# Norms whose epsilon comes from one more column: GpSimd keeps only the power

## The chip, the cores and the metric

The kernel runs on one core of one Trainium2 chip. The time is the device time of one launch in microseconds (us). The core has five engines that run their own streams of instructions and wait for each other by semaphores: TensorE (PE; its weight loads are PEld), VectorE (DVE), ScalarE (ACT), GpSimd (POOL) and SyncE (SP, which here only issues DMAs).

## The reference

256 tokens of 1,024 float32 channels go through a two-layer block (attention mixers and convolution-gated FFNs) and through a second block (gated delta rule, long convolution, FFN, a per-layer gate). What matters here are the RMS norms between them:

```python
def rms_norm(x, g):
    xf = x.astype(jnp.float32)
    y = xf * lax.rsqrt(jnp.mean(xf * xf, axis=-1, keepdims=True) + EPS)     # EPS = 1e-6
    return (y * g.astype(jnp.float32)).astype(x.dtype)

h = x
for layer in range(DEPTH):                                # 2 layers
    h = h + mixer(rms_norm(h, norm_mix_g[layer]))         # norms 0 and 2
    h = h + conv_gated_ffn(rms_norm(h, norm_ffn_g[layer])) # norms 1 and 3
h = rms_norm(h, norm_out_g)                               # norm 4
x = h + second_mixer(rms_norm_2(h, g_mix))                # norm 5
x = x + ffn(rms_norm_2(x, g_ffn))                         # norm 6
x = x + sigmoid(rms_norm_2(x, g_pl) @ w_pl_gate) * pl     # norm 7
return rms_norm_2(x, g_final)                             # norm 8
```

## The kernel before, in words

The tokens are two tiles of 128 (`t` = 0 and 1, `TT` = 2), with the tokens in the partitions of `x` and of `xn`, both `[128, 2, 1024]`. Every product is made from three matmuls (lines 1019 to 1021): each operand is kept as a rounded part (`whi`, `xhi`, `hhi`) and the rest (`wlo`, `xlo`, `hlo`). The weights come as a stream of slots from SyncE's queue into a ring `raw`; ScalarE rounds a slot into `whi` (line 1661), VectorE subtracts into `wlo` (line 2150). Each engine's program is written out in order by hand, and each instruction waits for events (semaphores of the dictionary `S`).

A norm `k` of tile `t` runs over four engines, in this order:

1. ScalarE: `square(k, t)` (line 1687) squares `x[:, t, :]` and sums into `sumsq[:, t]`. The squares themselves land in `xn`, which is free at that time, or for norm 4 in `junk_4`, a view of the convolution's tile `cv`.
2. GpSimd: `deviation(k, t)` waits for that, calls `rstd_of`, which makes `sumsq / 1024 + EPS` with a `tensor_scalar` (line 897), waits for its own semaphore (`link`), and raises it to the power -0.5 with a `tensor_tensor` (line 898) into `rstd[:, t]`.
3. VectorE: `normalize` (line 2176) writes `xn = x * rstd * gain` in two halves of 512 columns.
4. TensorE: `turn_norm` transposes `xn` in eight blocks of 128 (line 1035) into PSUM. ScalarE rounds them into `xhi` (line 1741), VectorE subtracts into `xlo` (line 2236), and the next product can begin. Around it TensorE runs filler matmuls of `ident` (`spin`, line 1026), a fixed number for each place.

Norm 0 stands behind the load of `x` at the start. Norms 1 and 3 (`norm_behind_out`) stand behind the output products of the mixers: both tiles become ready at the same time, tile 0 is normalized first. Norms 2, 4, 6 and 7 (`norm_behind_down`) stand behind down products that finish tile 0 first: its norm runs while TensorE is still at tile 1, and tile 1's norm runs while TensorE is at the next product of tile 0. Norm 5 is normed from norm 4's result with a second chain on GpSimd (`deviation_5`, lines 910 to 917), and for it `scale_x` (line 2253) rewrites `x`. Norm 8 is the last work; after it `xn` is stored tile by tile (line 874).

`rstd_of` has three other callers: `deviation_5`, the keys' layer norm and the norm of `pl`.

Of the kernel before, what the change touches and what calls it, by code (L numbers as in the profile page):

```python
# [274 lines left out]
class Event:  # L275
# [13 lines left out]


EVENTS = {

    "weights_high": "slot n's rounded weights are written",
    "weights_low": "slot n's remainders are written, its raw weights no longer needed",
# [298 lines left out]
def build(nc, dram, counted, stop=None):  # L593
# [7 lines left out]
    with ctx:  # L601
# [16 lines left out]
        raw = sb("raw", [P, RAW, SLOT])  # L618
        whi = sb("whi", [P, RING, SLOT], F32R)
        wlo = sb("wlo", [P, RING, SLOT], F32R)  # L620
        x = sb("x", [P, TT, D])
        xn = sb("xn", [P, TT, D])
        xhi = sb("xhi", [P, KT, TOK], F32R)
        xlo = sb("xlo", [P, KT, TOK], F32R)
        gain = sb("gain", [P, D])
# [13 lines left out]
        with ExitStack() as area:  # L639
            hhi = sb("hhi", [P, FT, TOK], F32R, area)  # L640
            hlo = sb("hlo", [P, FT, TOK], F32R, area)
            cv = sb("cv", [P, 2, 2, TOK], F32, area)
            sg = sb("sg", [P, 2, TOK], F32, area)
            hf = sb("hf", [P, 2, TOK], F32, area)
        with ExitStack() as area:
            temp = sb("temp", [P, 2, TT, 512], F32, area)
            rope_a = sb("rope_a", [P, 512], F32, area)
            rope_b = sb("rope_b", [P, 512], F32, area)
            v0 = sb("v0", [P, TT, 512], F32, area)
            v1 = sb("v1", [P, TT, 512], F32, area)  # L650
            fm = sb("fm", [P, 4, 4, TOK], F32, area)
            fmi = sb("fmi", [P, 3, TOK], F32, area)
            bias = sb("bias", [P, 8, 384], F32, area)
            picked = sb("picked", [P, TT, TOK], F32, area)
            score = sb("score", [P, TT, TOK], F32, area)
            rel = sb("rel", [P, 2, TOK], F32, area)
            prob = sb("prob", [P, 3, 3 * P], F32, area)
            probT = sb("probT", [P, 2, 3 * P], F32, area)
            mixed = sb("mixed", [P, 2, TT, 4 * HD], F32, area)
            mhi = sb("mhi", [P, KT, TOK], F32R, area)  # L660
            mlo = sb("mlo", [P, KT, TOK], F32R, area)
            ks = sb("ks", [P, 3, TT, 64], F32, area)
            key_mean = sb("key_mean", [P, TT], F32, area)
            key_var = sb("key_var", [P, TT], F32, area)
            key_rstd = sb("key_rstd", [P, TT], F32, area)
            index_w = sb("index_w", [P, TT, 4], F32, area)
            top8 = sb("top8", [P, 8], F32, area)
            gate = sb("gate", [P, 4, TT * 8], F32, area)
            lowest = sb("lowest", [P, 2, 4, TT], F32, area)
            total = sb("total", [P, 2, 4, TT], F32, area)  # L670
            sunk = sb("sunk", [P, 2, 4, TT], F32, area)
            inverse = sb("inverse", [P, 2, 4, TT], F32, area)
            nsink = sb("nsink", [P, 8], F32, area)
# [152 lines left out]

            return (i % 2, i // 2) if (layer, b) == ("odd", 0) else (i // 2, i % 2)

        junk_4 = cv[:, :, :, :].rearrange("p a m c -> p (a m c)")

        def summed(n, t):

            return S["weights_used"].at(n) if t else S["first_summed"].at(n)
# [26 lines left out]
        @block.sync  # L860
        def _(sp):
            sp.dma_start(ident, dram["ident"]).then_inc(ident_loaded, 16)
            for t in range(TT):
                sp.dma_start(x[:, t, :], dram["x"][t * P:(t + 1) * P, :]).then_inc(x_loaded[t], 16)
                if t == 0:
                    sp.dma_start(gain[:, :], dram["gains"][0:1, :].broadcast_to([P, D])).then_inc(gain_0_loaded, 16)
            for n in range(len(plan)):
                if n >= RAW:

                    sp.wait_ge(*weights_low(n - RAW))  # L870
                sp.dma_start(used(raw, n), weights_of(n, dram["stream"][n])).then_inc(weights_loaded[n % RAW], 16)
            for t in range(TT):
                sp.wait_ge(*S["normed"].at((NORMS - 1, t)))
                sp.dma_start(dram["out"][t * P:(t + 1) * P, :], xn[:, t, :]).then_inc(stored, 16)
            sp.wait_ge(stored, 16 * TT)


# [1 line left out]
        def _(pool):  # L879
# [20 lines left out]
            def deviation(k, t):  # L900

                pool.wait_ge(*S["squared"].at((k, t)))
                if k:
                    pool.wait_ge(*S["normed"].at((k - 1, t)))
                ins = rstd_of(rstd[:, t:t + 1], sumsq[:, t:t + 1], 1.0 / D, EPS)
                ins.then_inc(*S["rstd_ready"].one((k, t)))
                if k == 4:
                    pool.wait_ge(*S["rstd_ready"].at((k, t)))

# [8 lines left out]
            def norm(k):  # L918

                for t in range(TT):  # L920
                    deviation(k, t)

            link(pool.memset(half_power[:, :], -0.5))
            norm(0)
            pool.dma_start(cst1[:, :], dram["consts1"]).then_inc(consts_loaded, 16)
# [725 lines left out]
        def _(act):  # L1651
# [21 lines left out]
            def square(k, t):  # L1673

                if k == 0:
                    act.wait_ge(x_loaded[t], 16)
                elif k == 5:
                    act.wait_ge(*S["gained"].at((t, 1)))
                    act.activation(junk_4, xn[:, t, :], ACT.Square, accum_out=sumsq_5[:, t:t + 1])\
                        .then_inc(*S["squared"].one((5, t)))  # L1680
                    return
                else:
# [1 line left out]
                    act.wait_ge(*S["rstd_ready"].at((k - 1, t)))  # L1684

                    act.wait_ge(*S["norm_turned"].at(("o" if k == 6 else k - 1, t, 1)))
                act.activation(junk_4 if k == 4 else xn[:, t, :], x[:, t, :], ACT.Square, accum_out=sumsq[:, t:t + 1])\  # L1687
                    .then_inc(*S["squared"].one((k, t)))
                if k == 4:
                    act.wait_ge(*S["squared"].at((k, t)))  # L1690
# [1170 lines left out]
```

## Time and profile before

| | |
|---|---|
| median of three runs | 1335.07 us (1334.74 to 1338.38) |
| the profiled execution | 1332.6 us, span of its instructions 1330.8 us |
| busy in it | TensorE 97%, its weight loads 89%, VectorE 63%, ScalarE 53%, GpSimd 18% |
| chain that ended last, by engine | TensorE 89%, VectorE 5%, ScalarE 3%, GpSimd 0% (rounded) |
| line 1687, square of one tile, 1,024 columns | 1.06 us, its sum's read 0.19 us |
| line 897, scaled sum on GpSimd | 20 times, 18 of them on `sumsq` or `sumsq_5` |
| line 898, power on GpSimd | 20 times |
| line 2176, half of a tile of `xn` | 0.75 us |

The busy share of an engine alone does not say what a saved instruction is worth; for that the waits of the engine behind it are read, place by place. In the rows below a time is in microseconds from the span's start, and what stands in brackets behind an instruction is how long its engine sat idle before it and what ended that.

### The profile page before, as it was taken

The page shows a single profiled execution, that of the slowest core. Times are in us where ns is not written, and L with a number is a line of the kernel's source. Part 1 is how long each engine was busy: PE and PEld are TensorE (multiplying, and loading weights), DVE is VectorE, ACT ScalarE, POOL GpSimd, SP SyncE. Part 2 cuts the span into 40 slices and gives each one's busy share as a digit, 9 for nine tenths or more (in the row PEclk, how much of TensorE's full clock was granted, in tenths as well). Part 3 has the DMA queues.
Part 4 walks back from the last instruction along what each step waited for, and adds up shares of the span by engine and source line. Part 5 has one row for each costly group of instructions (what it writes and reads, how often), then busy time and mean ns, then how long its engine had stood idle before and what let it go on. Part 6 is the DMA issues. An engine that isn't in the chain of part 4 may idle for free.

```text
span 1330.8 us, 21614 instructions
## 1 busy us (share of the span) xinstructions
PE 1289.0 (97%) x8824; PEld 1179.5 (89%) x8824; DVE 840.3 (63%) x1454; ACT 703.6 (53%) x1161; POOL 241.9 (18%) x196
## 2 busy tenths in 40 slices
PE   8999999999999999999999999999899999999996
PEld 7777899998877789998889999999889989999875
DVE  6774487774664458776467787778843456555445
ACT  5555466553445546654355666666646335444344
POOL 2000000000000010000046665565435201000001
PEclk9999999999999999999989999999999999999999
DMA  8523355445442245545433322332202536455432
GB/s 317 215 100 122 112 190 177 178 179 182 164 152 102 89 176 219 185 175 198 143 127 127 128 96 98 125 126 97 96 33 98 182 139 216 182 190 189 175 143 79
DMA packets 31442, 200.29 MB, mean 151 GB/s; under 512 B 4272, under 2 KB 6464, under 8 KB 8560
## 3 DMA queue, kind: packets, MB, share of 16 engines
q1 hardware_dynamic: 29360, 189.79, 39.5%
q0 software_dynamic: 1840, 8.60, 1.6%
q8 instruction: 70, 1.15, 0.3%
q10 hardware_dynamic: 144, 0.52, 0.1%
q14 instruction: 28, 0.23, 0.1%
HBM read 197.85 MB, written 1.05 MB: 149 GB/s over the span
## 4 chain that ended last, share of the span: by engine, by line
PE 89%; DVE 5%; ACT 3%; issue 1%; DMA 0%; POOL 0%; SPq 0%; POOLq 0%; DVEq 0%; ACTq 0%
PE ps L1019 25%; PE ps L1021 24%; PE ps L1020 24%; PE ps L1174 2%; PE ps L1377 2%; PE ps L1142 1%; PE ps L1393 1%; DVE conv L2526 1%; PE ps L1035 1%; PE ps L1155 1%; PE ps L1333 1%; PE ps L1100 1%; DVE wlo L2150 1%; PE ps L1338 1%; PE ps L1399 1%
## 5 line engine op out<-in xcount | busy, mean ns | idle before, releaser
L1019 PE MATMUL ps<-xhi,whi 128*128 128x256 f32 x1536 | 441.3, 287 | 2.6 <-DVE xlo L2233 2.6
L1020 PE MATMUL ps<-xlo,whi 128*128 128x256 f32 x1536 | 436.3, 284 | 0.0
L1021 PE MATMUL ps<-xhi,wlo 128*128 128x256 f32 x1536 | 436.2, 284 | 0.0
L2150 DVE TENSOR_TENSOR wlo<-raw,whi 128x2048 fp32r<-128x2048 f32 (+2 forms) x144 | 324.7, 2257 | 124.5 <-ACT whi L1661 121.2
L1661 ACT ACTIVATE whi<-raw 128x2048 fp32r<-128x2048 f32 (+2 forms) x144 | 270.7, 1882 | 117.0 <-PE ps L1021 112.7
L1019 PEld LDWEIGHTS ps<-xhi,whi 128*128 128x128 f32 x1536 | 296.1, 193 | 2.9 <-DVE xlo L2233 2.8
L1020 PEld LDWEIGHTS ps<-xlo,whi 128*128 128x128 f32 x1536 | 296.1, 193 | 0.1
L1021 PEld LDWEIGHTS ps<-xhi,wlo 128*128 128x128 f32 x1536 | 295.8, 193 | 0.0
L977 POOL TENSOR_TENSOR wlo<-raw,whi 128x1024 fp32r<-128x1024 f32 x72 | 173.8, 2422 | 60.8 <-ACT whi L1670 60.5
L897 POOL TENSOR_SCALAR sumsq<-sumsq 128x1 f32<-128x1 f32 x18 | 5.8, 322 | 890.5 <-ACT xn L1687 700.9
L1019 PE MATMUL ps<-whi,xhi 128*128 128x512 f32 (+4 forms) x432 | 152.2, 352 | 4.0 <-DVE xlo L2236 3.4
L1021 PE MATMUL ps<-whi,xlo 128*128 128x512 f32 (+4 forms) x432 | 147.1, 341 | 0.0
L1020 PE MATMUL ps<-wlo,xhi 128*128 128x512 f32 (+4 forms) x432 | 146.9, 340 | 0.0
L1019 PE MATMUL ps<-whi,hhi 128*128 128x512 f32 x264 | 104.5, 396 | 0.9 <-DVE hf L2469 0.9
L1020 PE MATMUL ps<-wlo,hhi 128*128 128x512 f32 x264 | 104.4, 395 | 0.0
L1021 PE MATMUL ps<-whi,hlo 128*128 128x512 f32 x264 | 104.4, 395 | 0.0
L1019 PEld LDWEIGHTS ps<-whi,xhi 128*128 128x128 f32 x432 | 82.2, 190 | 19.9 <-issue 10.0
L2589 DVE SCALAR_TENSOR_TENSOR ps<-glu_in,par,ps 128x256 f32<-128x256 f32 x224 | 94.6, 482 | 0.0
L1833 ACT ACTIVATE cv<-ps,par 128x256 f32<-128x256 f32 x88 | 44.9, 561 | 89.6 <-PE ps L1021 83.2
L1021 PEld LDWEIGHTS ps<-whi,xlo 128*128 128x128 f32 x432 | 82.3, 191 | 9.3
L1020 PEld LDWEIGHTS ps<-wlo,xhi 128*128 128x128 f32 x432 | 82.5, 191 | 7.7
L1670 ACT ACTIVATE whi<-raw 128x1024 fp32r<-128x1024 f32 x72 | 76.1, 1060 | 11.8 <-PE ps L1021 11.8
(296 smaller groups left out, 1757.4 us busy)
## 6 DMA issues: line engine op xcount, KB each, us to landing
raw<-in_stream SPq DMA_DIRECT2D x176, 1024.0 KB, 4.8
gain<-in_gains POOLq DMA_DIRECT2D x7, 512.0 KB, 5.4
bias<-in_rel POOLq DMA_DIRECT2D x1, 1536.0 KB, 8.9
raw<-in_stream SPq DMA_DIRECT2D x2, 648.0 KB, 7.9
cst<-in_consts POOLq DMA_DIRECT2D x1, 1280.5 KB, 6.2
raw<-in_stream SPq DMA_DIRECT2D x2, 528.0 KB, 4.1
x<-in_x SPq DMA_DIRECT2D x2, 512.0 KB, 4.8
out<-xn SPq DMA_DIRECT2D x2, 512.0 KB, 2.6
```

The costliest lines, as they stand in the source:

```text
L977: pool.tensor_tensor(wlo[:, n % RING, c], raw[:, n % RAW, c], whi[:, n % RING, c].bitcast(F32), ALU.subtract).then_inc(*S["pool_weights_lo ...
L1019: nc.tensor.matmul(out, a_hi, b_hi, start=start, stop=False)
L1020: nc.tensor.matmul(out, a_hi, b_lo, start=False, stop=False)
L1021: return nc.tensor.matmul(out, a_lo, b_hi, start=False, stop=stop)
L1035: last = nc.tensor.transpose(ps[:, 4 + 2 * t + half, i * P:(i + 1) * P], xn[:, t, (4 * half + i) * P:(4 * half + i + 1) * P], ident)
L1174: last = nc.tensor.matmul(ps[:, bank, tile_logits(t)], q, k, start=True, stop=True)
L1377: last = nc.tensor.matmul(ps[:, PRODUCT_BANK[i], y * P:(y + 1) * P], turned[:, y, :], by[:, y, :], start=True, stop=True)
L1661: act.activation(used(whi, n), used(raw, n), ACT.Copy).then_inc(*S["weights_high"].one((n, 1)))
L1670: act.activation(whi[:, n % RING, c], raw[:, n % RAW, c], ACT.Copy).then_inc(*S["weights_high"].one((n, half)))
L1833: act.activation(cv[:, j % 2, m, :], ps[:, up_bank(j), m * TOK:(m + 1) * TOK], ACT.Identity, bias=par_at(f"conv_b{li}", c), scale=par_at(f ...
L2150: dve.tensor_tensor(used(wlo, n), used(raw, n), used(whi, n).bitcast(F32), ALU.subtract)\
L2589: dve.scalar_tensor_tensor(odd_taps[:, :] if k == 29 else sums, src, w, sums, ALU.mult, ALU.add)\
```

## The change

`x` and `xn` get a column more, `[128, 2, 1025]`. GpSimd sets that column of `x` once, at the start, to `(EPS * 1024) ** 0.5`. ScalarE's square reads 1,025 columns with a scale of `1024 ** -0.5`, so that its sum is the mean of the squares plus EPS. `deviation` no longer calls `rstd_of`: it issues only the power. Norm 5's square stays as it was, on 1,024 columns, and so do `deviation_5` and the other callers of `rstd_of`. `junk_4` becomes a tile of its own. The loads of `x` and the store of `xn` take 1,024 columns of rows that are now 1,025 long, and every tile that is allocated behind `x` begins at another address.

```diff
 EVENTS = {
+    "edge_set": "the columns of x whose square adds EPS to a mean",
@@
-        x = sb("x", [P, TT, D])
-        xn = sb("xn", [P, TT, D])
+        x = sb("x", [P, TT, D + 1])
+        xn = sb("xn", [P, TT, D + 1])
@@
+            junk_4 = sb("junk_4", [P, D + 1], F32, area)
@@
-        junk_4 = cv[:, :, :, :].rearrange("p a m c -> p (a m c)")
-
@@
-                sp.dma_start(x[:, t, :], dram["x"][t * P:(t + 1) * P, :]).then_inc(x_loaded[t], 16)
+                sp.dma_start(x[:, t, 0:D], dram["x"][t * P:(t + 1) * P, :]).then_inc(x_loaded[t], 16)
@@
-                sp.dma_start(dram["out"][t * P:(t + 1) * P, :], xn[:, t, :]).then_inc(stored, 16)
+                sp.dma_start(dram["out"][t * P:(t + 1) * P, :], xn[:, t, 0:D]).then_inc(stored, 16)
@@ def deviation(k, t):
                 pool.wait_ge(*S["squared"].at((k, t)))
                 if k:
                     pool.wait_ge(*S["normed"].at((k - 1, t)))
-                ins = rstd_of(rstd[:, t:t + 1], sumsq[:, t:t + 1], 1.0 / D, EPS)
-                ins.then_inc(*S["rstd_ready"].one((k, t)))
+                pool.tensor_tensor(rstd[:, t:t + 1], sumsq[:, t:t + 1], half_power[:, 0:1], ALU.pow).then_inc(*S["rstd_ready"].one((k, t)))
@@
+            pool.memset(x[:, :, D:D + 1], (EPS * D) ** 0.5).then_inc(*S["edge_set"].one())
             link(pool.memset(half_power[:, :], -0.5))
             norm(0)
@@ def square(k, t):
                 if k == 0:
                     act.wait_ge(x_loaded[t], 16)
+                    act.wait_ge(*S["edge_set"].at())
                 elif k == 5:
                     act.wait_ge(*S["gained"].at((t, 1)))
-                    act.activation(junk_4, xn[:, t, :], ACT.Square, accum_out=sumsq_5[:, t:t + 1])\
+                    act.activation(junk_4[:, 0:D], xn[:, t, 0:D], ACT.Square, accum_out=sumsq_5[:, t:t + 1])\
@@
-                act.activation(junk_4 if k == 4 else xn[:, t, :], x[:, t, :], ACT.Square, accum_out=sumsq[:, t:t + 1])\
+                act.activation(junk_4[:, :] if k == 4 else xn[:, t, :], x[:, t, :], ACT.Square, scale=D ** -0.5, accum_out=sumsq[:, t:t + 1])\
                     .then_inc(*S["squared"].one((k, t)))
```

## Rows read from the trace of the kernel before

**Rows 1.** The page: busy time by engine, and the last chain by engine.

```profile
PE 1289.0 (97%) x8824; PEld 1179.5 (89%) x8824; DVE 840.3 (63%) x1454; ACT 703.6 (53%) x1161; POOL 241.9 (18%) x196
...
PE 89%; DVE 5%; ACT 3%; issue 1%; DMA 0%; POOL 0%; SPq 0%; POOLq 0%; DVEq 0%; ACTq 0%
```

**Rows 2.** Waits of TensorE: us in total, times, the longest.

```profile
PE ps L1035 <- DVE xn L2176: 4.7, 4, 1.4
```

**Rows 3.** Lines 897 and 898, whole span: ns least/median/most, first and last start.

```profile
L897 POOL TENSOR_SCALAR sumsq<-sumsq x18: 182/192/980, 6.0 to 1324.9; 128x1 f32<-128x1 f32 x18
...
L898 POOL TENSOR_TENSOR rstd<-sumsq,half_power x18: 549/560/2463, 6.3 to 1325.4; 128x1 f32<-128x1 f32 x18
```

**Rows 4.** Timeline, norm 1, tile 0: start, us busy, engine, line, operation.

```profile
154.72 0.19 POOL L897 TENSOR_SCALAR sumsq<-sumsq 128x1 f32<-128x1 f32 x1 [115.32 <-ACT xn L1687]
...
155.00 0.57 POOL L898 TENSOR_TENSOR rstd<-sumsq,half_power 128x1 f32<-128x1 f32 x1
...
156.49 1.32 PE L1035 MATMUL ps<-ident,xn 128*128 128x128 f32 x8 [1.20 <-DVE xn L2176]
```

**Rows 5.** Timeline, norm 0, tile 1.

```profile
9.37 0.19 POOL L897 TENSOR_SCALAR sumsq<-sumsq 128x1 f32<-128x1 f32 x1 [2.49 <-ACT xn L1687]
9.65 0.55 POOL L898 TENSOR_TENSOR rstd<-sumsq,half_power 128x1 f32<-128x1 f32 x1
9.80 0.69 DVE L2236 TENSOR_TENSOR xlo<-ps,xhi 128x512 fp32r<-128x512 f32 x1 [1.39 <-ACT xhi L1741]
```

**Rows 6.** Timeline, norm 2, tile 1: weight loads of both halves' transposes.

```profile
355.51 0.42 PEld L1035 LDWEIGHTS ps<-ident,xn 128*128 128x128 f32 x4 [0.28 <-DVE xn L2176]
...
356.17 0.42 PEld L1035 LDWEIGHTS ps<-ident,xn 128*128 128x128 f32 x4 [0.24 <-DVE xn L2176]
```

**Rows 7.** Timeline, norms 4 and 5, tile 1; the last row is filler matmuls.

```profile
674.32 0.19 POOL L897 TENSOR_SCALAR sumsq<-sumsq 128x1 f32<-128x1 f32 x1 [7.63 <-ACT cv L1687]
674.37 2.28 DVE L2150 TENSOR_TENSOR wlo<-raw,whi 128x2048 fp32r<-128x2048 f32 x1
...
674.60 2.46 POOL L898 TENSOR_TENSOR rstd<-sumsq,half_power 128x1 f32<-128x1 f32 x1
...
675.53 4.27 PE L1026 MATMUL ps<-ident 128*128 128x128 f32 x20
```

**Rows 8.** Granted clock: the core's mean; one microsecond (0.50, third from the end).

```profile
core 0: 1330.8 us, clock 0.990
...
676.00:677.00 1.00, 1.00 (x7) 1.00 (x7) 0.65 (x1) 1.00 (x1) 1.00 (x1) 0.50 0.00 0
```

**Rows 9.** Timeline, norm 6, tile 1: second half's transposes.

```profile
1103.69 0.42 PEld L1035 LDWEIGHTS ps<-ident,xn 128*128 128x128 f32 x4 [0.25 <-DVE xn L2176]
```

**Rows 10.** Timeline, norm 7, tile 1.

```profile
1294.56 2.28 DVE L2150 TENSOR_TENSOR wlo<-raw,whi 128x2048 fp32r<-128x2048 f32 x1
...
1295.92 0.98 POOL L897 TENSOR_SCALAR sumsq<-sumsq 128x1 f32<-128x1 f32 x1 [9.84 <-ACT xn L1687]
...
1296.98 0.55 POOL L898 TENSOR_TENSOR rstd<-sumsq,half_power 128x1 f32<-128x1 f32 x1
...
1298.45 1.32 PE L1035 MATMUL ps<-ident,xn 128*128 128x128 f32 x8 [0.90 <-DVE xn L2176]
```

**Rows 11.** Timeline, norm 8: tile 0's `xn`, then tile 1.

```profile
1324.47 1.42 DVE L2176 SCALAR_TENSOR_TENSOR xn<-x,rstd,gain 128x512 f32<-128x512 f32 x2 [0.81 <-POOL rstd L898]
...
1325.35 0.94 POOL L898 TENSOR_TENSOR rstd<-sumsq,half_power 128x1 f32<-128x1 f32 x1
...
1326.32 1.41 DVE L2176 SCALAR_TENSOR_TENSOR xn<-x,rstd,gain 128x512 f32<-128x512 f32 x2 [0.44 <-POOL rstd L898]
```

**Rows 12.** Loads of `x` (line 864): least, median and most time to landing.

```profile
DMA to landing us min/median/max: 3.5/4.8/6.0
```

**Rows 13.** Groups by form, whole span: busy us, mean ns of one.

```profile
L1021 PE MATMUL ps<-whi,hlo 128*128 128x512 f32 x264 | 104.4, 395 | 0.0
...
L1021 PE MATMUL ps<-whi,xlo 128*128 128x512 f32 x224 | 87.7, 391 | 0.0
```

## The prediction

> **What bounds the kernel now.** I read the page's totals and its chain first: TensorE is busy for 97% of the span and carries 89% of the chain, GpSimd rounds to 0% of it [rows 1]. So an edit to GpSimd's two small instructions counts only where TensorE stands still for a norm, or behind TensorE's last product. The waits of TensorE say how much of that there is: it waited 4.7 us in 4 places for the normalized rows `xn` [rows 2]. The view of lines 897 and 898 then gives the two instructions that the change is about: the scaled sum (`TENSOR_SCALAR`, 0.19 us in the median) and the power (0.56 us) [rows 3]. After that I looked at every norm in the timeline, both tiles of tokens, and asked what TensorE (or, in norm 8, VectorE) was waiting for.
>
> Norm 1 is the clean pattern [rows 4]. ScalarE's square, the scaled sum at 154.72, the power at 155.00, and TensorE's transposes at 156.49 after 1.20 us of idle time. The scaled sum's part is the spacing of the two starts, 0.28 us.
>
> **What the change removes.** Sixteen scaled sums of norms 0 to 4 and 6 to 8 go, with the semaphore round trip behind each; the two of `deviation_5`, the one of the keys and the one of `pl` stay. The starts lie 0.27 to 0.28 us apart where nothing is in the way [rows 4, 5]. Sixteen times that is 4.4 us, but most places have other work over them:
>
> - Norm 0, both tiles: nothing. Tile 1's power ends at 9.65 + 0.55 = 10.20, but VectorE is at `xlo` of tile 0 from 9.80 for 0.69 us and starts tile 1's `xn` only then [rows 5]. Tile 0 is followed by ScalarE's square of tile 1, which waits for its own load.
> - Norm 1, tile 0: the whole 0.28, since TensorE is idle for 1.20 just before [rows 4]. Tile 1's transposes come behind tile 0's product: nothing.
> - Norm 2, tile 0 lies under the second half of the down product: nothing. Tile 1: the weight loads of the two halves' transposes waited 0.28 and 0.24 for `xn` [rows 6]. About 0.25 can be had before TensorE's own product is the bound.
> - Norm 3, tile 0: the same code and order as norm 1, 0.27.
> - Norms 4 and 5: nothing. Tile 0 lies under the product. In tile 1 TensorE runs 20 fixed filler matmuls (4.27 us from 675.53), at the clock's lower level of 1.2 GHz (granted 0.50) [rows 7, 8], and `xn` is ready as they end.
> - Norm 6, tile 1: TensorE comes to the first half's transposes as their input comes, so only the second half's wait of 0.25 can go [rows 9]. I take 0.24.
> - Norm 7, tile 1: TensorE was idle for 0.90. The scaled sum took 0.98 here, since it began inside VectorE's `wlo` (1294.56 + 2.28 = 1296.84) and ended 0.06 behind it; the power then ended at 1297.53 [rows 10]. The new power must wait for the same `wlo`. How long it then still needs shows in norm 4: the power at 674.60 began inside a `wlo` that ended at 674.37 + 2.28 = 676.65, and ended at 677.06, 0.41 behind it [rows 7]. So it ends here at 1296.84 + 0.41 = 1297.25 instead of 1297.53: 0.28.
> - Norm 8, tile 1, the last thing before the store: its power at 1325.35 ended at 1326.29, 0.40 behind tile 0's `xn` (1324.47 + 1.42 = 1325.89), and VectorE started tile 1 at 1326.32 [rows 11]. Tile 0's `xn` comes 0.28 earlier, and the power of tile 1 again ends 0.40 behind it: 0.28. If it finishes between VectorE's two halves instead, VectorE need not wait at all and the gap of 0.44 goes too, 0.72 in all. I take 0.28, since the old scaled sum and power both waited for VectorE there.
>
> The sum is 0.28 + 0.25 + 0.27 + 0.24 + 0.28 + 0.28 = 1.60 us.
>
> Of GpSimd the Trainium skill (Perfetto Trace Analysis, GPSIMD Engine Instruction) says that a reported duration is not to be trusted and that one should time by the spacing of starts. Reckoned by durations, the step would be worth 0.19 and the sum 1.1 us; the spacing of the starts [rows 4] is what I have used, and the two differ by 0.5 us here.
>
> **What it adds.** A `memset` of two columns goes to the start of GpSimd's queue, before the first power's wait: nothing can use it before `x` has landed, 3.5 us behind its issue at the least [rows 12], and GpSimd itself waits for the squares of `x`. So it is hidden many times over. ScalarE gets one more wait (`edge_set`) in norm 0; the two squares and everything ScalarE does are queued behind it, but it is long fulfilled; at most some hundredths of a microsecond. The square has 1,025 columns for 1,024 (1.06 us for 1,024 in the table above, so about 1 ns more) and a scale: nothing. What has no row is the new pitch. Tile 1 of `x` and `xn` now begins at an address that is only a multiple of 4 bytes, and `xhi`, `xlo`, `gain` and all tiles behind them move up. For engines I take nothing. For the load of `x`, which stands in front of norm 0, the two loads of before took 3.5 and 6.0 us [rows 12], so I bound the cost by 0 and 2.5 and take 0, as their difference comes with their place in the queue and not with the pitch, which was the same for both.
>
> **A wait that changes its owner.** In norm 4, tile 1, the scaled sum started at 674.32, VectorE's `wlo` at 674.37, and the power then stood until `wlo` was done [rows 7]. With the change the power stands at 674.32. The Trainium skill (SBUF — State Buffer, Who interferes with whom) says that a VectorE instruction with two inputs in SBUF and a GpSimd instruction that reads SBUF share a port, and that the one that starts first keeps it. The rows with 2.46 and 0.98 us agree. By it `wlo` would now wait for the power, up to 0.56 us, and `scale_x` behind it would start about where it did. From the rows alone: either the power passes under `wlo` and up to 0.44 of VectorE's wait goes, or VectorE is pushed back by at most 0.56; in the first case the fillers hide it, in the second `xn` is at most 0.1 us late, since the old one had also waited for the power. Zero in the sum, 0.1 in the range.
>
> **How it stands to the median.** The profiled execution took 1332.6 us with a span of 1330.8; the median of three is 1335.07. The sum is a difference, so I take it from the median: 1335.07 - 1.60 = 1333.5 us.
>
> **The rivals.**
>
> *A, the forecast:* six places give 0.24 to 0.28 each. Between 1.1 (durations) and 2.1 (norm 8 gives 0.72): 1333.0 to 1334.0, and to 1334.7 with small costs of the pitch. Chance 0.60.
>
> *B, the clock:* the granted clock was 0.990 in the mean and 0.50 in the microsecond from 676 [rows 8], so that 27 us in all (0.010 x 1330.8 / 0.5) went by at the lower level, in several stretches. Fillers cost 0.21 us apiece there (4.27 / 20). Shifts of some tenths of a microsecond can move a fall onto other work, or do away with one. A stretch about as long as the fillers (4.27 us) costs at most half of itself, so I take 1.7 for one. For it: the runs of before are 3.6 us apart. Against it: no gap of TensorE gets longer. One stretch less 1331.8, one more 1335.2. Chance 0.16, half each way.
>
> *C, the power is no quicker alone:* the change does less than it says. The power always follows another GpSimd instruction by 0.09 us; after an idle queue it may start that much later, so that the scaled sum had only covered a start-up. Against it: scaled sums behind over 100 us of idle time took 0.19 as those behind 2 us. Then the time is 1335.1. Chance 0.08.
>
> *D, TensorE reads its stationary tiles slower where they move to:* the slower side. Products with `whi` moving and `xlo` or `xhi` standing took 391 ns, those with `hlo` 395, for the same shape [rows 13]. The tiles have the same shape and steps but for the number of blocks; what else differs is their place. If the pitch gives `xhi` and `xlo` the worse place, 224 x 3 matmuls cost 4 ns more each, 2.7 us: 1335.07 - 1.60 + 2.7 = 1336.2, slower than before. It decides against the change from 2.4 ns per matmul on (1.60 / 672) and is outside of what can be measured from 8.3 ns on (1.60 + 4.0 over 672), or at once if the far more frequent 256-column products pay too. The other way round the 264 x 3 products with `hhi` would gain 3.2 us: 1330.3. For it: nobody else explains the 4 ns. Against it: all products with `xhi` sit at addresses of the same kind, and a shift of a few dozen bytes may leave them so. Chance 0.10, of which 0.07 slower and 0.03 faster.
>
> *E, the load or the store at the odd pitch is slower:* up to 2.5 us in front of norm 0 [rows 12]; with 1.3 on average 1334.8, at most 1336.0. Chance 0.06.
>
> **How the numbers follow.** The predicted time is A's, 1333.5. About a tenth on each side may be left out: below, a stretch of clock and norm 8's 0.72 together, 1331.2; above, D and E's end with a little of the spread of the runs, 1336.6. What a measurement of this kernel can tell from no change is about 0.3%, 4.0 us: faster means under 1331.06, slower over 1339.07. Faster needs D's good side or two stretches of clock less: 0.06. Slower needs D's bad side at more than twice the 4 ns, or two stretches more: 0.06. The rest, 0.88, is within.
>
> **What the changed profile would show.** Right: line 897 left with 4 instructions instead of 20; in norms 1 and 3 the power starts about 0.1 behind ScalarE's accumulator read, and TensorE's idle time before the transposes falls from 1.20 to about 0.92; in norm 7 from 0.90 to about 0.6; the waits for `xn` fall from 4.7 by about 1.1; the last `xn` starts 0.28 earlier behind the last square; norm 0's first product starts where it did, at 12.7. Wrong: a power that starts 0.37 behind ScalarE's read, not 0.1 (C), matmuls with `xlo` or `hlo` whose mean moves by 4 ns (D), a second tile of `x` that lands later than 8.1 (E), or a total that moves by more than 2 us with unchanged norms (B).

## The result and the profile after

| | before | after |
|---|---|---|
| median of 6 runs each | 1334.90 us (1329.98 to 1339.01) | 1319.55 us (1312.88 to 1324.02) |
| ratio | | 0.9872, interval 0.9841 to 0.9903 |
| profiled execution, its span | 1332.6, 1330.8 | 1313.9, 1312.1 |

The change made the kernel 15 us faster, and 1.6 had been forecast. The page says at once where they went. It gives busy time by engine (compare [rows 1]):

```profile
PE 1270.1 (97%) x8824; PEld 1158.3 (88%) x8824; DVE 839.8 (64%) x1454; ACT 703.3 (54%) x1161; POOL 238.3 (18%) x181
```

TensorE has the same 8,824 matmuls and is busy for 18.9 us less, as much as the span has lost (18.7). GpSimd has lost 3.6 us, and that is not the gain. The groups by form name the matmuls: busy us, mean ns of one. First three of before that [rows 13] doesn't hold, then those of after:

```profile
L1019 PE MATMUL ps<-xhi,whi 128*128 128x256 f32 x1536 | 441.3, 287 | 2.6 <-DVE xlo L2233 2.6
L1020 PE MATMUL ps<-xlo,whi 128*128 128x256 f32 x1536 | 436.3, 284 | 0.0
L1021 PE MATMUL ps<-xhi,wlo 128*128 128x256 f32 x1536 | 436.2, 284 | 0.0
```

```profile
L1019 PE MATMUL ps<-xhi,whi 128*128 128x256 f32 x1536 | 433.7, 282 | 2.6 <-DVE xlo L2234 2.6
L1020 PE MATMUL ps<-xlo,whi 128*128 128x256 f32 x1536 | 428.6, 279 | 0.0
L1021 PE MATMUL ps<-xhi,wlo 128*128 128x256 f32 x1536 | 428.4, 279 | 0.0
...
L1021 PE MATMUL ps<-whi,hlo 128*128 128x512 f32 x264 | 104.3, 395 | 0.0
...
L1021 PE MATMUL ps<-whi,xlo 128*128 128x512 f32 x224 | 88.4, 395 | 0.0
```

The three groups of 1,536 matmuls in which `xhi` or `xlo` is the moving operand (the first of the two names: 256 tokens of `xhi` stream past `whi`) took 5 ns less each. `whi,xlo`, the form that the prediction had looked at, went the other way, from 391 to 395 [rows 13].

A duration is the modelled end of a pipelined matmul; the start-to-start time is firmer. The timeline of TensorE in after (start, us busy):

```profile
199.83 0.28 PE L1019 MATMUL ps<-xhi,whi 128*128 128x256 f32 x1
199.94 0.28 PE L1020 MATMUL ps<-xlo,whi 128*128 128x256 f32 x1
200.06 0.28 PE L1021 MATMUL ps<-xhi,wlo 128*128 128x256 f32 x1
200.17 0.28 PE L1019 MATMUL ps<-xhi,whi 128*128 128x256 f32 x1
```

One triple (the three matmuls of one product, lines 1019 to 1021) takes 0.34 from its first start to the next one's. In before it took 0.36 (in the rounded starts below 0.37, in the record of that stretch 0.360 in 313 of 318 triples):

```profile
200.03 0.28 PE L1019 MATMUL ps<-xhi,whi 128*128 128x256 f32 x1
200.16 0.28 PE L1020 MATMUL ps<-xlo,whi 128*128 128x256 f32 x1
200.28 0.28 PE L1021 MATMUL ps<-xhi,wlo 128*128 128x256 f32 x1
200.40 0.28 PE L1019 MATMUL ps<-xhi,whi 128*128 128x256 f32 x1
```

Line 1019 in 100 us in the middle of layer 0's FFN, before and after (PE busy and count, PEld busy and count, granted clock, DMA share, GB/s):

```profile
180.00:280.00 100.00, 78.59 (x279) 53.35 (x278) 1.00 0.53 193
```

```profile
180.00:280.00 100.00, 81.18 (x295) 55.23 (x295) 1.00 0.56 203
```

279 triples against 295, at a granted clock of 1.00 in both and with no wait shown in the rows. So it is neither the clock nor a wait for another engine.

For finer sums I use GpSimd's powers of tile 0 as milestones; from one norm's to the next is a stretch of the program. In before they start at 155.00 [rows 4] and 343.39, in after at:

```profile
157.14 0.56 POOL L905 TENSOR_TENSOR rstd<-sumsq,half_power 128x1 f32<-128x1 f32 x1 [118.75 <-ACT xn L1688]
...
338.42 0.56 POOL L905 TENSOR_TENSOR rstd<-sumsq,half_power 128x1 f32<-128x1 f32 x1 [174.92 <-ACT xn L1688]
```

| stretch, us | before | after | difference |
|---|---|---|---|
| start to norm 1 | 155.00 | 157.14 | +2.1 |
| norm 1 to 2 (FFN, layer 0) | 188.39 | 181.28 | -7.1 |
| norm 2 to 3 (mixer) | 132.17 | 132.46 | +0.3 |
| norm 3 to 4 (FFN, layer 1) | 188.38 | 181.26 | -7.1 |
| norm 4 to 6 (second mixer) | 426.40 | 423.09 | -3.3 |
| norm 6 to 7 (FFN) | 195.17 | 191.27 | -3.9 |
| norm 7 to 8 | 38.29 | 38.39 | +0.1 |

The FFNs, with 320 triples of their first product (the up product) each, gained. The mixers of the two layers, where 512 columns of weights stream past a standing `xhi`, did not. In the traces of kernels with the same places and the same arithmetic (before, e6 and e16; e1 and e3; after and e10; e2 and e9), which come from several chips, the stretches 1 to 2, 3 to 4 and 6 to 7 agree to 0.02 us, but for one that differs by 0.13. The first and the fifth move by several us with the granted clock. That makes the three a better scale than the total.

### The profile page after: what moved, and what is told of

It is laid out like the page before. It is cut to its first block, busy times and chain, and to the rows that moved or that the text cites. A ratio compares the mean times of both kernels' runs of the same rounds, so it can differ in the third digit from the quotient of the medians.

```text
span 1312.1 us, 21601 instructions
## 1 busy us (share of the span) xinstructions
PE 1270.1 (97%) x8824; PEld 1158.3 (88%) x8824; DVE 839.8 (64%) x1454; ACT 703.3 (54%) x1161; POOL 238.3 (18%) x181
## 4 chain that ended last, share of the span: by engine, by line
PE 69%; issue 21%; DVE 5%; ACT 3%; DMA 1%; POOL 1%; SPq 0%; POOLq 0%; DVEq 0%; ACTq 0%
PE ps L1019 20%; PE ps L1020 19%; PE ps L1021 19%; PE ps L1377 1%; PE ps L1393 1%; DVE conv L2527 1%; PE ps L1333 1%; DVE xlo L2237 1%; DMA bias<-in_rel 1%; PE ps L1035 1%; PE ps L1399 1%; DMA x<-in_x 0%; ACT xhi L1742 0%; DVE wlo L2151 0%; PE ps L1338 0%
## 5 line engine op out<-in xcount | busy, mean ns | idle before, releaser
L1019 PE MATMUL ps<-xhi,whi 128*128 128x256 f32 x1536 | 433.7, 282 | 2.6 <-DVE xlo L2234 2.6
L1020 PE MATMUL ps<-xlo,whi 128*128 128x256 f32 x1536 | 428.6, 279 | 0.0
L1021 PE MATMUL ps<-xhi,wlo 128*128 128x256 f32 x1536 | 428.4, 279 | 0.0
L1019 PEld LDWEIGHTS ps<-xhi,whi 128*128 128x128 f32 x1536 | 290.6, 189 | 2.9 <-DVE xlo L2234 2.8
L1020 PEld LDWEIGHTS ps<-xlo,whi 128*128 128x128 f32 x1536 | 290.7, 189 | 0.1
L1021 PEld LDWEIGHTS ps<-xhi,wlo 128*128 128x128 f32 x1536 | 290.1, 189 | 0.0
L905 POOL TENSOR_TENSOR rstd<-sumsq,half_power 128x1 f32<-128x1 f32 x16 | 12.3, 770 | 879.5 <-ACT xn L1688 696.9
L1670 ACT ACTIVATE whi<-raw 128x1024 fp32r<-128x1024 f32 x72 | 76.1, 1060 | 11.8 <-PE ps L1021 11.8
```

The lines of the kernel that those rows point to most:

```text
L1019: nc.tensor.matmul(out, a_hi, b_hi, start=start, stop=False)
L1020: nc.tensor.matmul(out, a_hi, b_lo, start=False, stop=False)
L1021: return nc.tensor.matmul(out, a_lo, b_hi, start=False, stop=stop)
L1670: act.activation(whi[:, n % RING, c], raw[:, n % RAW, c], ACT.Copy).then_inc(*S["weights_high"].one((n, half)))
```

## The experiments

Two theories. **A**, the prediction's: the 16 scaled sums are worth something, and layout nothing. **L**: what counts is where `xhi` and `xlo` lie against the weight tiles. The program's memory is handed out in multiples of 32 bytes, so that rows of 1,025 columns move `xn` by 32 bytes and `xhi` and everything behind it by 64; `raw`, `whi`, `wlo` and `x` stay.

Totals scatter by some 3 us because of the clock, which the record of each execution gives. Through 79 executions of the kernel before, on four chips, runs a line: 1334.28 us at a mean granted clock of 0.989, and 1.04 us less for each 0.001 more; single executions lie 0.75 us off it (standard deviation). An eightieth is left out: its record has a clock of 0.940 at 1336.36 us, where the line would have 1385. "At equal clock" below is the mean distance of a kernel's executions from this line, with two standard errors.

**e1, the arithmetic without the layout.**

```diff
-                ins = rstd_of(rstd[:, t:t + 1], sumsq[:, t:t + 1], 1.0 / D, EPS)
-                ins.then_inc(*S["rstd_ready"].one((k, t)))
+                pool.tensor_tensor(rstd[:, t:t + 1], sumsq[:, t:t + 1], half_power[:, 0:1], ALU.pow).then_inc(*S["rstd_ready"].one((k, t)))
@@ square: scale=D ** -0.5
```

> Only the arithmetic of the change, on the tiles and addresses of before: ScalarE squares with a scale of 1024 ** -0.5, GpSimd only raises to the power; the epsilon of norms 0 to 4 and 6 to 8 is left out. Theory L (the tiles' new addresses made TensorE faster): only the saved scaled sums count, 1.6 us off 1335 (1333.3), ratio 0.998 to 1.000; triples of matmuls with 256 moving columns stay 0.36 us apart, mean 284 ns for one of line 1020. Theory T (the shorter chain did it, by the clock or by what runs beside it): a ratio near 0.988 and 279 ns.

Measured: 1333.13, ratio 0.9999 (0.998 to 1.0018); at equal clock -2.5 ± 0.3 us. Its triples take 0.36, its group `xhi,whi` 288 ns. So the arithmetic is about a sixth of the gain. The stretches, by the milestones, are 188.11, 131.83, 188.10, then 194.88 and 37.80: 0.28, 0.34, 0.28, 0.29 and 0.49 less than before.

**e5, the layout without the arithmetic:** `x` and `xn` get the 1,025 columns, everything else is left.

```diff
-        x = sb("x", [P, TT, D])
-        xn = sb("xn", [P, TT, D])
+        x = sb("x", [P, TT, D + 1])
+        xn = sb("xn", [P, TT, D + 1])
@@ the loads, the store and the squares take 0:D
```

> x and xn with 1,025 columns as in the change, but the arithmetic of before on the first 1,024. Theory L1 (only the place of xhi and xlo counts): as with 64 unused bytes, ratio 0.994, triples 0.35 apart. Theory L2 (the pitch of x and xn, or the 32 bytes by which xn itself moves, counts as well): near the changed kernel, 0.988 to 0.990, triples 0.34 apart in the first part. Theory M (the power and the place only act together): 0.994, and the rest of the gain comes from neither alone.

Measured: 1320.19, ratio 0.9882 (0.9851 to 0.9913), at equal clock -14.5 ± 3.0. Stretches 181.55 and 181.55, that is 6.8 less than before each; with e1's 0.28 that is the changed kernel's 181.28 and 181.26. The two parts add up. GpSimd's 16 scaled sums are all back in this kernel, and its interval holds the changed kernel's 0.9872.

**e2, only a gap of 64 bytes in front of `xhi`.**

```diff
         xn = sb("xn", [P, TT, D])
+        pad_1 = sb("pad_1", [P, 16])
```

> The kernel before with one unused tile of 64 bytes behind xn, so that xhi and all behind it stand where the change put them; nothing else differs. Theory L: ratio about 0.988 to 0.990 (some 15 us less, without the 1.6 of the scaled sums), matmuls with xhi moving 279 ns instead of 284, those with xlo standing and 512 moving columns 395 instead of 391. Theory T: no change, 0.999 to 1.001, 284 ns.

Measured: 1326.29, ratio 0.9944 (0.9923 to 0.9965), -9.0 ± 0.5 at equal clock. An unused tile of 64 bytes, and 9 us. But not the some 15 that had been expected: line 1020 (the first of the triple, one line further down here) ran 284 times in the 100 us, where it had run 279 and 295 times:

```profile
180.00:280.00 100.00, 78.96 (x284) 52.92 (x283) 1.00 0.56 198
```

A triple takes 0.353 (in layer 0 211 of 318 triples took 353 ns and 105 took 354), a spacing between the other two. Some expectations below write 0.3506 for this spacing; from start to start of whole triples it is 0.353.

**e3, the changed kernel with `xhi` moved by 4,096 bytes instead of 64** (a gap of 4,032 bytes behind `xn`).

> The changed kernel with an unused tile of 4,032 bytes behind xn, so that xhi and all behind it move by 4,096 bytes against before and not by 64. Theory L, if what counts is the address modulo some power of two up to 4,096: the gain goes, ratio 0.998 to 1.000, 284 ns and 391 ns. Theory T: 0.988 stays.

Measured: 1334.98, ratio 1.0009 (0.9984 to 1.0035), -2.3 ± 0.6 at equal clock. The change's whole code is in it, the odd rows too, and what is left is e1's 2.5. Its stretches 188.12, 131.84 and 188.10 are e1's. Without the place the longer rows and the arithmetic bring no more than e1, and the place counts with a period that divides 4,096.

**e6, 64 bytes in front of `raw`**, so that all tiles move together.

> The kernel before with 64 unused bytes in front of raw, so that every tile moves by the same 64 bytes. If what counts is how xhi and xlo stand to whi and wlo (the standing tile is loaded while the moving one is read), nothing changes: 1.000 and 0.36. If the address itself counts: as with 64 bytes behind xn, 0.994 and 0.35.

Measured: 1335.42, ratio 0.9993 (0.9972 to 1.0015), +0.3 ± 0.6 at equal clock, stretches 188.40 and 188.39. It is the distance between tiles that counts, not the address: that of `xhi` and what lies behind it to `raw`, `whi`, `wlo`, `x` or `xn`. The up products read `whi` and `wlo` of these; but `raw`, `whi` and `wlo` moved together in every run, and VectorE, ScalarE and the DMAs write them at the same time, so that no run shows which of the three tiles, or whose access, it is.

**e16, a gap of 2,048 bytes behind `xn`.**

> The kernel before with 2,048 unused bytes behind xn, so that the distance of xhi and xlo to whi and wlo changes by 2,048. Theory L with a period of 4,096 bytes or a finer one: if the period is 2,048 or a divisor, all spacings are those of the kernel before (0.360 and 0.680) and the ratio is 1.000; if it is 4,096, they differ, by something between -1.4% and +1%.

Measured: 1335.87, ratio 0.9997 (0.9975 to 1.002), 0.0 ± 0.6, stretches 188.39 and 188.38: the period divides 2,048.

**e4, a gap of 128 bytes; e7, 64 bytes between `xhi` and `xlo`; e8, a gap of 32 bytes.**

> The kernel before with 128 unused bytes behind xn. Theory L with a period of 64 bytes: nothing differs from before or everything does as with 64; with a period of 128: as before, 284 ns and 1.000; with a longer one: a third value. Theory T: 1.000, 284 ns.

> The kernel before with 64 unused bytes between xhi and xlo, so that xlo and all behind it move and xhi does not. Relative theory: only pairs of instructions in which xlo takes part get quicker, one matmul of three moves xlo; a third to two thirds of the 8.6 us of 64 bytes behind xn, ratio 0.996 to 0.998, triples 0.352 to 0.357.

> The kernel before with 32 unused bytes behind xn. A conflict between two readers that depends on the distance in steps of 64 bytes or more: as before, 1.000 and 0.36. A finer one: another value, between 0.34 and 0.36.

| kernel | `xhi` moved by | triple, up (layer 0, layer 1) | 512 columns past `xhi` | past `hhi` | norm 1 to 2, 3 to 4 | total | at equal clock |
|---|---|---|---|---|---|---|---|
| before | 0 | 0.360, 0.360 | 0.685 | 0.701 | 188.39, 188.38 | 1334.9 | 0 |
| e8 | 32 | 0.350, 0.350 | 0.699 | 0.686 | 183.61, 183.62 | 1317.97 | -14.4 ± 0.9 |
| e2 | 64 | 0.353, 0.353 | 0.700 | 0.700 | 185.93, 185.94 | 1326.29 | -9.0 ± 0.5 |
| e4 | 128 | 0.356, 0.356 | 0.698 | 0.702 | 187.23, 187.23 | 1331.38 | -1.7 ± 0.3 |
| e7 | 0, `xlo` 64 | 0.360, 0.360 | 0.693 | 0.700 | 188.13, 188.12 | 1333.70 | -1.9 ± 0.6 |

(Triples are means of the times from the start of one triple to the start of the next, worked out from the traces, without those over a tenth longer than the shortest, which hold the breaks between blocks.) The ratios are 0.9857 (0.9826 to 0.9888) for e8, 0.9973 (0.9953 to 0.9994) for e4 and 0.9975 (0.9957 to 0.9994) for e7. e4 is the third value that its expectation had for a period longer than 128. e7's total is in its range and its up triples are not: they were to be 0.352 to 0.357 and stayed at 0.360, and what it gained came elsewhere (its triples of 256 weight columns past `xhi` in the FFNs took 0.354 for 0.360). No place is best for all forms: where `xhi` as the moving operand is quick, it is slow as the standing one. Of these kernels only e8 has the products with `hhi` quicker too, 391 ns for 395:

```profile
L1019 PE MATMUL ps<-whi,hhi 128*128 128x512 f32 x264 | 103.3, 391 | 0.9 <-DVE hf L2469 0.9
L1021 PE MATMUL ps<-whi,hlo 128*128 128x512 f32 x264 | 103.2, 391 | 0.0
```

**Why 0.34?** e2 and e5 have `xhi` and all behind it at the same addresses, and gained 9.0 and 14.5 us. **e9** is e2 again and **e10** the changed kernel again, on another chip; **e11** has 32 bytes in front of and 32 behind `xn`, so that `xn` too is where the change has it, with rows of 1,024; **e12** is the changed kernel with `xhi` moved by 4,128, which by the period is e8's place.

> The kernel before with 64 unused bytes behind xn once more, beside the changed kernel on the same chip. If the difference between 0.994 (64 bytes) and 0.988 (the change) belongs to the layout: 0.994 and 0.35 again, steady. If it belongs to the chip or the execution: nearer to the changed kernel's.

> The changed kernel once more. 0.987 to 0.989, triples 0.34 apart in the first part, if the layout sets them.

> The kernel before with 32 unused bytes between x and xn and 32 behind xn: xn and xhi stand exactly where the change puts them, only the pitch of x and xn stays 4,096 bytes. If xn's own place makes the rest of the gain: 0.988 and 0.34. If the pitch does: 0.994 and 0.35.

> The changed kernel with 4,064 unused bytes behind xn, so that xhi and all behind it move by 4,128 bytes. If distances 4,096 apart are alike (0 and 4,096 were), this is the kernel with 32 unused bytes plus the saved scaled sums: 1318 less 1.6, some 1316, ratio 0.984 to 0.986, hhi products 391 ns; the fastest so far.

Measured: e9 1323.51, 0.9900 (0.9868 to 0.9933), -8.6 ± 1.0, triples 0.353. e10 1316.04, 0.9848 (0.9813 to 0.9884), stretches 181.28 and 181.27. e11 1325.33, 0.9918 (0.9887 to 0.9948), -8.1 ± 0.5, stretches 185.95 and 185.95: the place of `xn` does nothing. e12 1317.62, 0.9863 (0.983 to 0.9896), stretches 183.32 and 183.32, which is e8 less 0.29. So the two spacings repeat from chip to chip. Of what differs between e2 and the changed kernel, the length of the rows of `x` and `xn` was left.

**e13 to e15: 1,025 columns in `x` alone, in `xn` alone, and 1,028 in both**, each with every tile from `xhi` on at +64.

> The kernel before with a row of 1,025 columns in x alone; xn keeps 1,024, and 32 unused bytes behind it put xhi and all behind it at +64 bytes, as in the changed kernel. Theory L1 (it is the odd pitch of x that makes the first part's triples 0.340 instead of 0.3506): triples of 0.340 before 600 us, ratio 0.986 to 0.988 to the kernel before. Theory L2 (it is the pitch of xn): triples of 0.3506 everywhere, ratio about 0.992. Theory L3 (either alone does it): 0.340 here and in the run with xn alone.

> The same with the 1,025 columns in xn alone and x at 1,024, every tile from xn on at the place that it has in the changed kernel. L2 (xn's pitch): triples of 0.340 before 600 us and a ratio of 0.986 to 0.988; L1 (x's pitch): 0.3506 and 0.992.

> x and xn with rows of 1,028 columns: every tile begins where it does in the changed kernel, but token tile 1 begins at a multiple of 16 bytes instead of 4. If what counts is that tile 1 is at an address that is odd to some larger unit (the misalignment), the triples are 0.3506 and the ratio is about 0.992; if any pitch other than 4,096 bytes does it, 0.340 and 0.986 to 0.988.

No theory came out as written. e13: 1322.82, 0.991 (0.9879 to 0.9942). e14: 1316.29, 0.9859 (0.9822 to 0.9895). In the profiled execution of both, layer 0 had 0.340 and layer 1 had 0.353, in one execution at the same addresses. In e13, line 1019 in 100 and in 80 us:

```profile
180.00:280.00 100.00, 81.15 (x295) 55.22 (x295) 1.00 0.57 204
500.00:580.00 80.00, 63.16 (x227) 42.38 (x227) 1.00 0.54 194
```

The changed kernel had 236 in the second window, e2 227. The stretches are 181.69 and 185.94 in e13, 181.55 and 186.08 in e14. e15 (1317.83, 0.9888, interval 0.9847 to 0.9928) had 0.353 in both layers when profiled, but that was its slowest execution, 1326.95; the three others took 1317.6 to 1317.9. At equal clock the profiled executions lie 8.4 us (e15, neither layer quick), 14.2 and 14.2 (e13, e14, one layer) and 18.9 us (e5, both) under the kernel before: some 5 us a layer, against 4.4 between 185.93 and 181.55. Of the ten others of these three kernels seven lie within about a microsecond of one of these levels and three between two of them. So at this place TensorE has **two spacings, 0.340 and 0.353**. The choice between them would also explain most of the changed kernel's spread, 11 us over six runs, where e2's eight spread over 1.3.

The traces say more about when it chooses. The stream of an up product has short breaks (triples of some 0.43 us, after the first, the eighth and, in the last FFN, the 95th). Between two breaks the spacing at this place did not change, and at a break it could. In all six layer FFNs with 0.340 (of after, e5 and e10) and in layer 0 of e13 and e14 the six triples between the first and the second break took 0.353 and the 310 behind it 0.340. In the last FFN of after the spacing went back at the third break; 86 triples of 340 ns stand before it and 222 of 353 or 354 behind it. Line 1019 in 30 us before it and in 30 behind it, 88 matmuls and 86:

```profile
1100.00:1130.00 30.00, 24.12 (x88) 16.33 (x87) 1.00 0.58 211
1140.00:1170.00 30.00, 23.68 (x86) 15.96 (x85) 1.00 0.50 176
```

Nor do the longer rows own the quick spacing. e2 has rows of 1,024 columns, and its products of 256 weight columns past `xhi` in the FFN of layer 0 ran at 0.34 before a break and at 0.35 behind it:

```profile
163.04 0.28 PE L1020 MATMUL ps<-whi,xhi 128*128 128x256 f32 x1
...
163.38 0.28 PE L1020 MATMUL ps<-whi,xhi 128*128 128x256 f32 x1
...
169.13 0.28 PE L1020 MATMUL ps<-whi,xhi 128*128 128x256 f32 x1
...
169.48 0.28 PE L1020 MATMUL ps<-whi,xhi 128*128 128x256 f32 x1
```

**e17, e1's arithmetic with e2's gap:** the change without its longer rows.

> The arithmetic of e1 (epsilon is left out) with xhi and all behind it at +64 bytes by 64 unused bytes, rows of x and xn at 1,024 columns: the change without its pitch. At an equal granted clock e1 is 2.5 us under the kernel before and e2 9.0. Theory P (the faster form of the up products, 0.340 a triple, comes only where a row of x or xn is longer than 1,024 columns): triples of 0.3506 in both layers in every execution, 11.5 us under before at an equal clock, ratio about 0.991, and executions that lie as close together as those of e2. Theory S (it is decided by when and how the stretch starts, and the pitch had only moved that): some executions have 0.340 in one or both layers, and lie 5 or 10 us lower than that.

Measured: 1321.6, ratio 0.9893 (0.9872 to 0.9914), -10.6 ± 0.7 against 11.5 expected; triples of 0.353 in both layers, stretches 185.67 and 185.79, all five executions within 2.3 us at equal clock. The shift in time that the arithmetic brings did not call up 0.340 in a layer; in the last FFN the trace has it for the triples between the first and the second break, and not behind it. With e2, e9 and e11 that makes 23 executions with rows of 1,024 columns, and none of them lies more than 10.3 us under the line (e17's 2.5 taken off), where one quick layer would make it 13 to 14; of the 27 executions of the kernels with longer rows at this place (after, e5, e10, e13 to e15), 23 lie more than 11.8 under it. So the longer rows make the quick spacing far more frequent where it pays most, behind the second break of an up product, without being its condition. Why they do, though TensorE doesn't read `x` or `xn` while it is at the up products, stays open, and so does what decides at a break.

**e18, the changed kernel with 4,064 bytes behind `gain`:** `hhi` comes to e8's place, `xhi` stays.

> The changed kernel with 4,064 unused bytes behind gain: xhi and xlo stay at +64 bytes, hhi and hlo move to +4,128, which is +32 by the period of 4,096. Theory L holds for the standing tile hhi by itself: its triples of 512 columns take 0.680 instead of 0.700 as in e8, 264 x 0.02 = 5.3 us less, ratio to the kernel before about 0.983, and the up products stay at 0.340 or 0.3506 as in the changed kernel. Rival (hhi gains only together with xhi at +32): 0.700, and the time of the changed kernel, 0.987.

Measured: 1314.77, ratio 0.9839 (0.9818 to 0.986), executions from 1310.61 to 1315.56. The products with `hhi` take 391 ns and 0.680 a triple in the two layers (0.697 in the last FFN, where they took 0.703 in before), so each tile's place counts by itself:

```profile
L1019 PE MATMUL ps<-whi,hhi 128*128 128x512 f32 x264 | 103.3, 391 | 0.9 <-DVE hf L2470 0.9
```

Both layers had 0.353 when profiled. It has the lowest median of all, but the interval overlaps those of the changed kernel (0.9841 to 0.9903, and 0.9813 to 0.9884 in e10); that it beats it is likely and not shown.

## Why the prediction was wrong

**The step that failed** is one sentence: "For engines I take nothing", said of the new pitch and of all tiles that move. The movement of `xhi` by 64 bytes was worth 9 us and, with stretches at 0.340, 14 to 19, and the norms, the whole of the forecast, 2.5.

**Rival D had the mechanism and not the term.** It said that the place of a tile changes TensorE's speed, and priced it from the one pair of rows that showed such a difference, 391 and 395 ns for a *standing* `xlo` and `hlo`. That part came as priced: `whi,xlo` went to 395, and the 224 triples cost 0.009 to 0.019 more each with their breaks, 2.8 us in all where D had 2.7. The far more frequent 256-column products, which it named in half a sentence and gave no price, moved in the opposite direction: 640 triples of the two layers by 0.020 (12.6 us), 576 of the second mixer by 0.007 (4.1) and 320 of the last FFN by 0.010 (3.3), 20.0 us in all. Another 2 came from the 160 triples of 256 weight columns past `xhi`. Less 2.8 that is about 19 for the profiled execution, where 17.9 arrived at equal clock once e1's 2.5 are taken off. Its "against it", that a shift of a few dozen bytes may leave the products as they are, was wrong: 32, 64 and 128 bytes gave three different speeds, and 2,048 and 4,096 none.

The trace of before did hold a hint. 256 columns at 2.4 GHz last 0.1067 us, and the matmuls started 0.120 apart: 13 ns each that no column accounts for, 4,608 times, 61 us. 512 columns last 0.2133, and the starts were 0.228 (`xhi` standing) and 0.234 apart (`hhi`): 15 and 20 ns. In after they are 7 ns in the two layers, and 20 and 20. An excess that differs between operands of one shape is a hint that their place counts, which e18 then showed for `hhi`, and its largest holder is what to put a price on. The Trainium skill (TensorE: Matmul & The Clock Gate, Back-to-back issue gap) gives 262 cycles for 256 columns and 518 for 512 at 2.4 GHz, for a matmul by itself; as an estimate from that page a triple would take 0.328 and 0.648, which no stretch of any kernel here reached. The same page (Step-by-step: what each phase is for) says that loading the next weights takes no read bandwidth from the running matmul, as each has a port of its own. e2 and e6 make it doubtful for this kernel: a distance between tiles counted, and of the tiles in front of `xhi` TensorE reads only `whi` and `wlo` in an up product, which it loads. No run shows which access stands in the way of which, so the mechanism below the spacing stays open.

**A, the norms, was right place by place**, and can now be measured better than by totals:

| step | forecast | measured |
|---|---|---|
| norm 1, idle before the transposes | 1.20 to 0.92 | 0.90; stretch in e1 -0.28 |
| norm 2, tile 1 | 0.25 | the wait of 0.28 is gone, the second, 0.24, stands; stretch -0.34 |
| norm 3 | 0.27 | 1.19 to 0.91; stretch -0.28 |
| norm 6 | 0.24 | the wait of 0.25 is gone; stretch -0.29 |
| norm 7, idle | 0.90 to 0.6 | 0.64 in after, 0.62 in e1; stretch to norm 8 -0.49 |
| norm 8, last square to last `xn` | 0.28 | 2.63 to 2.35: 0.28 |

Transposes of norms 1 and 7 in after, against [rows 4, 10]:

```profile
158.62 1.32 PE L1035 MATMUL ps<-ident,xn 128*128 128x128 f32 x8 [0.90 <-DVE xn L2177]
...
1279.41 1.32 PE L1035 MATMUL ps<-ident,xn 128*128 128x128 f32 x8 [0.64 <-DVE xn L2177]
```

TensorE's waits for `xn` in norms 1, 3 and 7 fell from 3.29 to 2.45 us (2.43 in e1), by 0.84 where their three terms are 0.83. Their total, 4.7 in before [rows 2], is 3.6 in e1 and 4.4 in after: the difference is norm 0, which waited 1.42 in before, 1.17 in e1 and 0.35 + 1.61 in after. The "about 1.1" of the prediction's last part was not reached in after for that reason. The measured pieces are 0.28 + 0.34 + 0.28 + 0.29 + 0.49 + 0.28 = 1.96 where 1.60 was forecast. The excess is in norms 2 (0.09), 6 (0.05) and the stretch behind norm 7 (0.21), and is not located further; nor is the rest up to 2.5 ± 0.3. e1's interval of the ratio, 0.998 to 1.0018, is 5 us wide: without the clock and the milestones it could not be told from nothing, as the prediction had said of such a size.

Norm 8's rule, that the power ends 0.40 behind tile 0's `xn`, held: `xn` ended at 1305.75 + 1.41 = 1307.16 and the power at 1307.57, where VectorE again waited 0.44 (compare [rows 11]):

```profile
1305.75 1.41 DVE L2177 SCALAR_TENSOR_TENSOR xn<-x,rstd,gain 128x512 f32<-128x512 f32 x2 [0.53 <-POOL rstd L905]
...
1306.49 1.08 POOL L905 TENSOR_TENSOR rstd<-sumsq,half_power 128x1 f32<-128x1 f32 x1 [0.85 <-ACT xn L1688]
...
1307.60 1.42 DVE L2177 SCALAR_TENSOR_TENSOR xn<-x,rstd,gain 128x512 f32<-128x512 f32 x2 [0.44 <-POOL rstd L905]
```

**The wait that changes its owner**, norm 4, tile 1 (compare [rows 7]):

```profile
662.79 0.55 POOL L905 TENSOR_TENSOR rstd<-sumsq,half_power 128x1 f32<-128x1 f32 x1 [7.62 <-ACT junk L1688]
662.85 2.28 DVE L2151 TENSOR_TENSOR wlo<-raw,whi 128x2048 fp32r<-128x2048 f32 x1
...
663.42 1.76 POOL L912 TENSOR_TENSOR rstd<-rstd 128x1 f32<-128x1 f32 x1
```

The power began 0.06 before `wlo` and took 0.55, and `wlo` began inside it and took its usual 2.28: VectorE was not pushed back. GpSimd's next instruction, which began inside `wlo`, then stood until `wlo` had ended at 665.13. Of the rule that the prediction cited from the Trainium skill (SBUF — State Buffer, Who interferes with whom), this trace bears out the half in which GpSimd waits, and shows VectorE not waiting. `scale_x` came 2.20 behind the start of `wlo` where it had come 2.72 behind, and the fillers hid that, but for 0.17: from the first filler to the end of the transposes 5.42 became 5.25. The prediction had put zero there.

**B, the clock,** was not it: 0.989 against 0.990 in the profiled executions, and 1.00 in both in the windows above. It has a part in the first stretch, which was 2.1 us longer: the 96 triples of 512 columns past `xhi` there took 0.7250 for 0.7144 in the mean, breaks included, which is 1.0, and of the 30 us from 100 on, 6% less were granted than in before (27.91 us busy in both), at most 1.8. First before, then after:

```profile
100.00:130.00 30.00, 27.91 (x150) 1.00 0.36 135
```

```profile
100.00:130.00 30.00, 27.91 (x140) 0.94 0.40 140
```

**C** was wrong: powers start 0.09 behind ScalarE's read of the sum (1304.61 + 0.19 = 1304.80, then 1304.89), as scaled sums did. **E** was wrong: the second tile of `x` landed after 6.2 us, and in e1, with even rows, after 6.2 as well, where before had 6.0 [rows 12]. Norm 0's first product started at 12.90, and at 12.86 in e1, not at 12.71: 0.15 to 0.19 late, but with no part of the pitch in it: e3, with odd rows, had 6.0 and 12.74. Line 897 is left with 4 instructions, one each for `key_var` and `pl` and two for `deviation_5`.

## What to carry to other kernels

A change in the shape of one tile is a change in the place of all tiles behind it. Before crediting or blaming the edit, run its layout without its arithmetic, and the edit with the old place restored by an unused tile; here these two separated 14 us from 2.5. And divide the start-to-start time of the commonest matmul by its columns: what is left over was 61 us here, more than the 42 us in which TensorE was idle, and a gap of 32 bytes gave back a quarter of it.

## What the runs showed of the hardware

- The spacing of back-to-back matmuls depends on the distance between tiles, here that of `xhi` and `xlo` to the tiles in front of them, `whi` and `wlo` among these: for 256 columns past `whi` and `wlo`, 0.360 a triple at 0, 2,048 and 4,096 bytes of added distance, 0.350 at 32, 0.353 or 0.340 at 64, 0.356 at 128. For 512 columns of weights past `xhi`, 0.685 at 0, 0.699 at 32 and 0.700 at 64. Per matmul these are 13, 10, 11 or 7, and 12 ns over the columns' own time, and 15, 20 and 20.
- At 64 bytes two spacings (0.340 and 0.353) are possible. One is kept from one break of the stream to the next, in the layers' up products for over 100 us; one execution can have both, in two layers (e13, e14) or within one FFN (after, e10). Rows of 1,024 columns had the quick one too, but in the layers' up products it was seen only with longer rows. What selects it is open.
- The mean granted clock in an execution's record accounts for most of the spread between the executions of before: 1.04 us for 0.001, with 0.75 us left over in 79 of 80.
- A VectorE instruction with two inputs (`wlo`) that started 0.06 us behind GpSimd's power took its usual 2.28 us; GpSimd's next instruction, of some 0.2 us elsewhere, took 1.76 and ended with `wlo`.
